# Memory attention of a two-layer decoder trunk: the query projection from eight block products to seven

## What is computed

```
def memory_cross_attention(h, mem_n, wq, wkv, wo):
    q = (h @ wq).reshape(B, S, 4, 256)
    k, v = jnp.split(mem_n @ wkv, 2, axis=-1)
    s = jnp.einsum('bshd,bmhd->bhsm', q, k) * 256 ** -0.5
    p = jax.nn.softmax(s, axis=-1)
    o = jnp.einsum('bhsm,bmhd->bshd', p, v).reshape(B, S, D)
    return o @ wo
```

## Time and profile before

| | us |
|---|---|
| median of 3 executions | 5332.19 |
| lowest and highest | 5331.96 and 6007.23 |
| the profiled execution, its own time | 5337.37 |
| span of its slowest core (core 6) | 5335.7 |
| spans of the 8 cores | 5321.6 to 5335.7 |
| mean granted TensorE clock | 0.990 to 0.992 of full speed |

### The profile page before, as it was taken

How to read it: one execution, slowest core, us unless ns; L and a number is a source line. 1 busy time by engine, 2 the same in 40 slices (tenths; PEclk the granted TensorE clock), 3 DMA queues, 4 the chain that set the end, 5 groups by cost and what they waited for, 6 DMA issues and landing times.

```text
span 5335.7 us, 88324 instructions; the slowest of 8 cores (5321.6 to 5335.7 us)
## 1 busy us (share of the span) xinstructions
PE 5160.5 (97%) x28390; PEld 2518.4 (47%) x28912; DVE 3730.7 (70%) x5951; ACT 2425.6 (45%) x3944; POOL 1043.1 (20%) x1521
## 2 busy tenths in 40 slices
PE   7999999999999999999989999999999999899998
PEld 3445564444444444444444455544444444444443
DVE  7767675776867746667777676757768767556677
ACT  4327784433423465432443277844324235654233
POOL 2004451100100234100220044511001003331001
PEclk9999999999999999999999999999999999999999
DMA  6323222222222283123543222312222223921233
GB/s 131 52 40 57 34 43 41 44 44 40 41 48 37 50 147 73 28 40 49 122 112 55 45 55 33 52 27 44 46 39 41 48 37 57 153 56 25 41 59 95
DMA packets 97615, 304.61 MB, mean 57 GB/s; under 512 B 10896, under 2 KB 10896, under 8 KB 93072
## 3 DMA queue, kind: packets, MB, share of 16 engines
q0 software_dynamic: 84096, 251.70, 28.7%
q1 hardware_dynamic: 13072, 47.22, 2.7%
HBM read 533.76 MB, written 16.78 MB: 103 GB/s over the span
## 4 chain that ended last, share of the span: by engine, by line
PE 87%; DVE 4%; issue 3%; ACT 3%; POOL 1%; DMA 1%; SPq 0%; DVEq 0%; ACTq 0%; POOLq 0%
PE ps L681 38%; PE ps L747 21%; PE ps L1189 4%; PE ps L870 4%; PE ps L857 4%; PE ps L1014 3%; PE ps L1112 2%; PE ps L1261 2%; PE ps L564 2%; PE ps L1201 1%; PE ps L883 1%; PE ps L899 1%; DVE hn_tok L560 1%; DMA h<-x 1%; ACT junk L535 1%
## 5 line engine op out<-in xcount | busy, mean ns | idle before, releaser
L681 PE MATMUL ps<-arena 128*128 128x512 bf16 x9640 | 2166.6, 380 | 36.7 <-ACT arena L685 10.6
L681 PEld LDWEIGHTS ps<-arena 128*128 128x128 bf16 x9856 | 959.4, 98 | 1184.8 <-issue 59.0
L747 PE MATMUL ps<-arena 128*128 128x512 bf16 x5523 | 1242.2, 379 | 5.7
L749 DVE SCALAR_TENSOR_TENSOR h<-ps,h 128x512 f32<-128x512 f32 x1536 | 1025.6, 686 | 103.8 <-PE ps L747 81.4
L685 ACT ACTIVATE arena<-ps 128x512 f32<-128x512 f32 x1056 | 608.9, 588 | 1073.3 <-PE ps L681 1073.0
L688 DVE TENSOR_TENSOR arena<-ps,arena 128x512 f32<-128x512 f32 (+1 forms) x1056 | 723.9, 690 | 334.9 <-ACT arena L685 203.3
L691 ACT ACTIVATE arena<-arena 128x512 bf16<-128x512 f32 x704 | 442.7, 629 | 1031.5 <-DVE arena L688 1027.4
L747 PEld LDWEIGHTS ps<-arena 128*128 128x128 bf16 x5632 | 549.2, 98 | 658.9 <-issue 4.6
L592 POOL DMA_DIRECT2D arena<-ffn_w_in x192 | 103.9, 541 | 1821.7 <-PE ps L681 1483.9
L535 ACT ACTIVATE junk<-h 128x1024 bf16<-128x1024 f32 x288 | 303.9, 1055 | 288.7 <-DVE h L595 178.3
L734 DVE TENSOR_TENSOR arena<-ps,arena 128x512 bf16<-128x512 f32 x352 | 242.8, 690 | 238.7 <-PE ps L681 237.6
(11 more groups left out here) (134 smaller groups left out, 4697.9 us busy)
## 6 DMA issues: line engine op xcount, KB each, us to landing
arena<-ffn_w_in POOLq DMA_DIRECT2D x192, 512.0 KB, 5.2
arena<-ffn_w_out POOLq DMA_DIRECT2D x192, 256.0 KB, 5.6
arena<-conv_tp POOLq DMA_DIRECT2D x62, 512.0 KB, 8.2
h<-x SPq DMA_DIRECT2D x32, 512.0 KB, 11.4
arena<-hgrn_w_in POOLq DMA_DIRECT2D x64, 256.0 KB, 4.9
arena<-xattn_wkv POOLq DMA_DIRECT2D x16, 1024.0 KB, 10.8
y<-arena SPq DMA_DIRECT2D x32, 512.0 KB, 3.3
arena<-xattn_wq POOLq DMA_DIRECT2D x8, 1024.0 KB, 15.4
```

The lines of the kernel that those rows point to most:

```text
L681: P.op("pe", lambda e, bank=bank, k=k: e.matmul(psb(bank), lhsT=u.ap[:, slot * 512 + k * 128:slot * 512 + (k + 1) * 128], rhs=x[0][:, k, : ...
L747: P.op("pe", lambda e, j=j, wo=wo, act=act: e.matmul(psb(bo), lhsT=act.ap[:, t8 * 128:(t8 + 1) * 128], rhs=wo.ap[:, half * 512:(half + 1) ...
L749: P.op("dve", lambda e: e.scalar_tensor_tensor(out=h[:, tt, half * 512:(half + 1) * 512], in0=psb(bo), scalar=0.5, in1=h[:, tt, half * 512 ...
```

## The change

`qproj` gives way to `qpair(p)`, which projects two token blocks at once. With features and inputs each cut in two halves, the eight block products for two token blocks become seven, each over 4 groups of 128 inputs: 4 chunks of 7 x 4 = 28 matmuls, 112 for two blocks where 128 stood. For this

- VectorE forms four combinations of activation blocks per pair (`tbq[0]`, the upper half of the second block in place, `tbq[1]`, `tbq[2]`; 128x2048 bf16 each) and four combinations of weight blocks per chunk (`mixq`, 128x512 bf16 each);
- ScalarE takes three snapshots per chunk and copies one bank to `qT`; VectorE adds a snapshot to a bank three times per chunk;
- the weights come in chunks of 512 KB (bf16) through two buffers `wqu`, eight loads a stage (the four chunks of wq twice); chunk i + 2 is loaded when chunk i has been used up;
- `tbq` and two of the five snapshot buffers lie on the bytes of `wkv[0]` and `wkv[1]`: `tbq[0]` and `tbq[1]` on `wkv[0]`, `tbq[2]` and the two snapshots on `wkv[1]`. They can be written once the value products (L844 before, L852 now) have read those buffers;
- `qT` holds two blocks. `qpair(0)` is written ahead of block 0, `qpair(1)` behind the heads of block 1; behind the heads of blocks 0 and 2 no projection stands any more.

```
-            xa_wq_d = din("xattn_wq", [2, 2, 128, KC * 512])
+            xa_wq_d = din("xattn_wq", [2, 4, 128, 2048])
...
+            base = wkv[0].off
+            tbq = [ABuf(arena, base + j * 4096, 4 * 512, BF16) for j in range(3)]
+            snap += [ABuf(arena, base + 12288 + j * 2048, 512, F32) for j in range(2)]
...
+            def load_q(i):
+                if i < 2 * NB:
+                    wload(wqu[i % 2].ap[:, 0:2048], wq_d[i % 4], wqu[i % 2].keys(0, 2048))
+            load_q(0)
+            load_q(1)
...
-            def qproj(blk):
+            def qpair(p):
+                t0, t1 = 2 * p, 2 * p + 1
+                b11, b12, b21, b22 = x_half(0, t0), x_half(0, t1), x_half(1, t0), x_half(1, t1)
+                for o, i0, i1 in ((tb[0], b12, b11), (b12, b22, b12), (tb[1], b22, tb[0]), (tb[2], b21, tb[1])):
+                    P.op("dve", lambda e, o=o, i0=i0, i1=i1: e.tensor_tensor(out=o[0], in0=i0[0], in1=i1[0], op=ALU.subtract), reads=i0[1] + i1[1], writes=o[1], d=1220)
+                xs = {1: b11, 2: b21, 3: b22, 4: tb[2], 5: tb[0], 6: tb[1], 7: b12}
...
+                for c in range(5):
+                    if c < 4:
+                        mixq(q["u"])
+                        prod(q, 1, q["A"], True)
+                        snp(q["A"], q["s"][0])
+                    if m:
+                        prod(m, 7, m["A"], False)
+                        snp(m["A"], m["s"][2])
+                    if q:
+                        prod(q, 5, q["E"], True)
+                    if m:
+                        addq(m["E"], m["s"][2], dst(m["c"] + 4, 1))
+                    if q:
+                        prod(q, 2, q["B"], True)
+                        addq(q["B"], q["s"][0], dst(c, 0))
+                        prod(q, 6, q["A"], False)
+                        snp(q["A"], q["s"][1])
+                    if m:
+                        prod(m, 4, m["A"], False)
...
+                        prod(m, 3, m["E"], False)
+                        addq(m["E"], m["s"][1], dst(m["c"], 1))
+                        load_q(4 * p + m["c"] + 2)
+                    m = q
...
-            qproj(0)
+            qpair(0)
...
-                if blk + 1 < NB:
-                    qproj(blk + 1)
+                if blk % 2 == 1 and blk + 1 < NB:
+                    qpair((blk + 1) // 2)
```

More of the change, by code:

```diff
@@ L851, in emit_xattn, with mixq, q, prod @@
             xi = [0]
-            def qproj(blk):
[L854 to L862, removed]
+            def qpair(p):
+                t0, t1 = 2 * p, 2 * p + 1
+                tb = [(q.ap.rearrange("p (k n) -> p k n", n=512), q.keys()) for q in tbq]
+                b11, b12, b21, b22 = x_half(0, t0), x_half(0, t1), x_half(1, t0), x_half(1, t1)
+                for o, i0, i1 in ((tb[0], b12, b11), (b12, b22, b12), (tb[1], b22, tb[0]), (tb[2], b21, tb[1])):
+                    P.op("dve", lambda e, o=o, i0=i0, i1=i1: e.tensor_tensor(out=o[0], in0=i0[0], in1=i1[0], op=ALU.subtract), reads=i0[1] + i1[1], writes=o[1], d=1220)
+                xs = {1: b11, 2: b21, 3: b22, 4: tb[2], 5: tb[0], 6: tb[1], 7: b12}
+                slot = {1: 0, 2: 1, 3: 6, 4: 2, 5: 4, 6: 5, 7: 3}
+                def mixq(u):
+                    def q(i):
+                        return u.ap[:, i * 512:(i + 1) * 512], u.keys(i * 512, (i + 1) * 512)
+                    for o, i0, i1, op in ((4, 3, 2, ALU.add), (5, 4, 0, ALU.subtract), (3, 0, 3, ALU.subtract), (6, 1, 5, ALU.subtract)):
+                        P.op("dve", lambda e, o=o, i0=i0, i1=i1, op=op: e.tensor_tensor(out=q(o)[0], in0=q(i0)[0], in1=q(i1)[0], op=op), reads=q(i0)[1] + q(i1)[1], writes=q(o)[1], d=425)
+                def prod(st, n, bank, start):
+                    u, x = st["u"], xs[n]
+                    for k in range(4):
+                        P.op("pe", lambda e, k=k: e.matmul(psb(bank), lhsT=u.ap[:, slot[n] * 512 + k * 128:slot[n] * 512 + (k + 1) * 128], rhs=x[0][:, k, :], start=(start and k == 0), stop=(k == 3), skip_group_check=not start),
+                             reads=u.keys(slot[n] * 512, (slot[n] + 1) * 512) + x[1], writes=psk(bank), brk=(k == 0))
+                def snp(bank, z):
+                    P.op("act", lambda e: e.activation(out=z.ap, in_=psb(bank), func=AF.Copy), reads=psk(bank), writes=z.keys())
+                def dst(c, j):
+                    return qTv[:, c, j * 512:(j + 1) * 512], qT.keys(c * 1024 + j * 512, c * 1024 + (j + 1) * 512)
+                def addq(bank, z, o):
+                    P.op("dve", lambda e: e.tensor_tensor(out=o[0], in0=psb(bank), in1=z.ap, op=ALU.add), reads=psk(bank) + z.keys(), writes=o[1])
+                m = None
+                for c in range(5):
+                    q = None
+                    if c < 4:
+                        i = 4 * p + c
+                        q = dict(c=c, u=wqu[i % 2], A=P.bank(), B=P.bank(), E=P.bank(), s=[snap[(3 * i + j) % 5] for j in range(3)])
+                        mixq(q["u"])
[15 more added lines that the diff above has]
+                        prod(m, 4, m["A"], False)
+                        o = dst(m["c"] + 4, 0)
+                        P.op("act", lambda e, m=m, o=o: e.activation(out=o[0], in_=psb(m["A"]), func=AF.Copy), reads=psk(m["A"]), writes=o[1])
+                        prod(m, 3, m["E"], False)
+                        addq(m["E"], m["s"][1], dst(m["c"], 1))
+                        load_q(4 * p + m["c"] + 2)
+                    m = q
```

20 lines of the change are left out of this document (11 added, 9 removed).

## The result

The changed kernel takes 5365.89 us (median of five executions, lowest 5361.97) against 5332.19: 33.7 us more. The ratio is 1.0063, with a 95% interval of 1.0043 to 1.0082. That is slower, by less than the 2% that were taken as the measure, and 6 us above the upper end of the predicted range.

What follows compares the result with a forecast made beforehand. TensorE, busy for 97% of the span, was taken to bound the kernel. The terms -27.6 + 10.5 + 3.8 + 5.4 + 2.4 + 3 + 6 = +3.5 us on the median of 5332.2 gave 5336 us, range 5313 to 5360.

Steps and rivals of the forecast that it cites:

- the ring of two: Query products waiting for wq chunks through two buffers: 0.6 us in half of the 8 pairs, 2.4 us in all.
- the heads: Attention heads standing alone without query products, TensorE waiting for Exp: 1.5 us a stage, 6 us in all.
- What the change removes: Query products on TensorE: 128 matmuls fewer at 0.216 us each, 27.6 us less.
- The value weights: Layer 1, TensorE waiting for piece 2 of wkv before the first value product: 6.4 and 4.1 us, together 10.5.
- the gain comes through: Rival: loads land sooner because wq's loads are half as large, and other fillers suffice; -17 us, 5315 us, chance 0.25.
- The first combination: Layer 1, TensorE waiting for VectorE to form `tbq[0]` after the value products: 1.9 us a stage, 3.8 in all.
- The clock: Layer 1, TensorE's granted clock falling around a wait of 4 to 6 us: 5.4 us for two stages.
- Layer 0's entry: End of the recurrence, where VectorE's added combinations meet additions to `h` and norms: 1.5 us a stage, 3 in all.
- have no price of their own: VectorE's combinations waiting for chunk loads, with operations queued behind: TensorE needs those no sooner than the chunk, no cost.
- The softmax as a bound: Rival: in the heads, Exp, ones and values with one buffer per parity become the bound; +45.5 us, 5378 us, chance 0.13.
- The clock in the heads: Rival: repeated short waits halve the clock for about 28 us of each stage; 112 us more, 5448 us, chance 0.02.

Runs made afterwards that it cites:

- e7: e6 plus a third buffer, on the second half of wo's bytes, for chunk 2 of the first pair; median 5313.6 us, ratio to before 0.9966.
- e8: The edits of e4 and e2 together in the changed kernel; median 5336.9 us, ratio to before 1.0001.
- e5: e2 plus the weight combinations of a stage's first two chunks put behind the last key product; median 5334.5 us, ratio to before 1.0005.
- e6: e5 plus bytes of their own for pieces 2 and 3 of wkv in layer 1; median 5318.3 us, ratio to before 0.9973.
- e2: The changed kernel with wo's two loads issued behind the load of chunk 3 of wq; 5339.59 us, one execution.
- e4: The changed kernel with the old eight block products by pair, without combinations, snapshots or additions; 5341.58 to 5346.05 us, ratio to before 1.0019.
- e1: The changed kernel with wo's two loads issued behind piece 3 of wkv; 5355.91 to 5360.44 us, ratio to before 1.0045.

## Why the prediction was wrong

The sign was right (+3.5 us), the size was not: +33.7. The step that failed is *the ring of two* with *the heads*, in layer 0. For chunk 2 of wq it took 5.2 us, the landing of the FFN's loads; behind wo's two loads chunk 2 took 16.6 and 15.2. By the stage table layer 0 gave back 25.5 us where the sum had 7.2 (its entry, and half of the ring and of the heads), layer 1 30.6 where it had 23.9. By its steps:

*What the change removes* holds. 896 products are left of 1024, and e7 lies 23 us under e8, of the 27.6, with the reservation made there.

*The value weights* were the right place, the size short: 7.31 + 7.89 = 15.2 us for 10.5. TensorE arrived 8.7 us after the issue, nearly as forecast (8.8 and 8.9); the loads took 15.9 and 16.4 us and not 15.2 and 13.0. The rival "the gain comes through" was answered rightly: wq's loads were through, by the DMA share of 0.23 at 2065 to 2070, and smaller ones free no time. But neither there nor in the sum was it asked which loads stand ahead of piece 2. They were wo's two, which TensorE needs only behind the heads.

*The first combination*: 4.3 us for 3.8. *The clock* in layer 1: the value products took 6.15 + 4.75 - 2 x 3.62 = 3.7 and 6.56 + 5.12 - 7.24 = 4.4 us more, 8.1 for 5.4.

*The ring of two and the heads* failed as one. While chunk 2 was missing, TensorE had only heads to do in layer 0. In the first sequence this cost 7.62 us of gaps, and behind them 13.20 us for 52 products (11.4 at 0.216) and 15.45 for 64 (13.98 in the same stage later), 3.3 us by the clock: 10.9 us where 0.6 + 1.5 stood in the sum. In the second it cost 5.35 us of gaps, and nothing by the clock on this core. For layer 1, where the heads were expected to stand alone, no wait of that kind came: the longest there for an Exp is 0.32 us.

*Layer 0's entry and VectorE.* TensorE's waits for a norm (L564 on L560) rose from 3.6 and 2.5 us a layer-0 stage to 5.0 and 4.6, near the 1.5 in the sum. With the gaps above this names 12.3 of the 13.9 us and 7.5 of the 11.6 (rows of the slowest core, means over all); the rest is not traced. That VectorE's combinations wait for loads and "have no price of their own" does not hold at the entry of layer 1: 4.8 us of VectorE's time, 1.5 of TensorE's, by the additions to `h` queued behind. What that cost the stage is open, since e5 took the wait away and did not clearly shorten it.

*The rivals.* The gain did come through, at the 5315 us given for it, but only in kernels whose loads are in time (e6 and e7: 5311 to 5321), and by other edits than the smaller loads. The softmax as a bound is refuted by e2, where the waits for Exp go with the buffer still shared. The clock in the heads: the granted clock was 0.92 at the gaps of the first sequence, 0.79 right behind them and 0.83 behind the last, with 1.00 between; in the second it was 1.00 behind gaps of 1.45 and 1.83. The rule from the Trainium skill ("TensorE: Matmul & The Clock Gate", "A second HAM failure mode: psum-queue depth-cycling") is borne out in kind by the first sequence, at 3.3 us in place of 28, and not by the second.

## What to carry to other kernels

When work is taken away that hid a load, list every load that stands ahead of it in the queue, whatever tensor it is for, and order the issues by when each is needed. A gap that the trace puts down to one engine may lie inside a longer wait for something else: look at what TensorE turns to when the gaps end. In a fixed order, an operation that waits for a load holds up everything behind it; put it behind what is already there.

## What was not expected of the hardware

The time from issue to landing followed what was issued ahead more than the load's own size: 512 KB took 5.7 us in e2 and 15.2 to 19.5 behind two loads of 1024 KB (the changed kernel, e4); 1024 KB took 8.9 in e1 and 15.9 behind them. The Trainium skill, "DMA: Bandwidth & Descriptors", section "Two DMAs through the same engine are not ordered", says that within one queue of a DMA engine descriptors start in order; these times agree. They do not settle everything: in e2 piece 2 took 10.9 and 11.8 us with none of wo ahead, and what held it is not shown.

Two waits of 2.15 and 2.08 us with four matmuls between them came ahead of a granted clock of 0.50 in e1 (stretch 2105 to 2110); behind one of 0.30 it was 1.00. Gaps of 1.35, 1.83 and 0.98 in the heads were followed by 0.79, gaps of 1.45 and 1.83 in the same place of the second sequence by 1.00.
